# Adaptive-norm parts of one row instead of two at the head of a fused decoder step, one Trainium2 core

## The reference, cut to what matters

```python
mod = (jax.nn.silu(c) @ w_ada + b_ada)[:, None, :]      # w_ada (1024, 6 * 1024)
sh1, sc1, gt1, sh2, sc2, gt2 = jnp.split(mod, 6, axis=-1)
h = rms_norm(x, g1) * (1 + sc1) + sh1
z = h @ w_in                                            # u, q, k, v, ga, gb
u, q, k, v, ga, gb = jnp.split(z, IN_SPLITS, axis=-1)
# pooling branch on u, windowed attention on q, k, v, both gated, @ w_out
x = x + gt1 * (merged @ w_out)
h2 = rms_norm(x, g2) * (1 + sc2) + sh2
x = x + gt2 * (jnp.square(jax.nn.relu(h2 @ w_up)) @ w_down)
```

## Time and profile before

| | |
|---|---|
| median of three runs | 1281.45 us (1281.41 to 1281.77) |
| profiled execution | 1281.86 us |
| its span, first to last instruction | 1280.1 us |
| mean granted TensorE clock | 0.998 of full speed |
| TensorE busy | 98% of the span |
| VectorE, ScalarE, GpSimd busy | 70%, 44%, 15% |
| moved by DMA | 211.61 MB, 165 GB/s in the mean |

### The profile page before, as it was taken

The page is one execution under the profiler, slowest core; times in us unless marked ns, Lnnn a source line. Parts: engine busy times, 40 slices in busy tenths (PEclk is TensorE's granted clock), DMA queues, the critical chain, the costliest instruction groups (busy, mean ns, idle before and its releaser), DMA issues. The chain is left out here.

```text
span 1280.1 us, 25027 instructions
## 1 busy us (share of the span) xinstructions
PE 1254.5 (98%) x10261; PEld 1226.1 (96%) x10261; DVE 895.3 (70%) x1354; ACT 565.2 (44%) x982; POOL 193.4 (15%) x185
## 2 busy tenths in 40 slices
PE   6999999999999999999999999999999999999997
PEld 5999999999888999999999999999999999999996
DVE  6766655788775544347888886767678975688864
ACT  6433222254435333336856565545463434333252
POOL 2000002000000222221453333233210000000021
PEclk9999999999999999999999999999999999999999
DMA  9982343211125764454445554354598666776533
GB/s 325 328 278 67 101 141 116 81 37 59 47 64 176 233 216 134 146 148 117 132 128 183 156 156 155 126 166 126 183 333 281 199 204 198 221 251 193 182 122 102
DMA packets 241950, 211.61 MB, mean 165 GB/s; under 512 B 17489, under 2 KB 224213, under 8 KB 236957
## 3 DMA queue, kind: packets, MB, share of 16 engines
q1 hardware_dynamic: 240972, 209.67, 51.8%
q10 hardware_dynamic: 865, 0.36, 0.1%
HBM read 161.97 MB, written 49.04 MB: 165 GB/s over the span
## 5 line engine op out<-in xcount | busy, mean ns | idle before, releaser
L692 PE MATMUL psum<-xh,b_lo 128*128 128x264 f32 x908 | 257.8, 284 | 0.0
L690 PE MATMUL psum<-xh,b_hi 128*128 128x264 f32 x908 | 256.7, 283 | 0.0
L691 PE MATMUL psum<-xl,b_hi 128*128 128x264 f32 x908 | 256.2, 282 | 0.0
L690 PE MATMUL psum<-dh,e_hi 128*128 128x264 f32 x896 | 255.0, 285 | 0.0
L691 PE MATMUL psum<-dl,e_hi 128*128 128x264 f32 x896 | 253.9, 283 | 0.0
L692 PE MATMUL psum<-dh,e_lo 128*128 128x264 f32 x896 | 253.7, 283 | 0.0
L691 PEld LDWEIGHTS psum<-xl,b_hi 128*128 128x128 f32 x908 | 170.5, 188 | 0.0
L690 PEld LDWEIGHTS psum<-xh,b_hi 128*128 128x128 f32 x908 | 170.4, 188 | 0.0
L692 PEld LDWEIGHTS psum<-xh,b_lo 128*128 128x128 f32 x908 | 170.1, 187 | 0.0
L691 PEld LDWEIGHTS psum<-dl,e_hi 128*128 128x128 f32 x896 | 168.9, 188 | 0.0
L690 PEld LDWEIGHTS psum<-dh,e_hi 128*128 128x128 f32 x896 | 168.8, 188 | 0.0
(11 more groups left out here) (365 smaller groups left out, 2741.2 us busy)
## 6 DMA issues: line engine op xcount, KB each, us to landing
down_raw<-in_w_down_dram SPq DMA_DIRECT2D x72, 512.0 KB, 5.7
dr<-ff_scratch SPq DMA_DIRECT2D x28, 1056.0 KB, 8.3
up_raw<-in_w_up_dram SPq DMA_DIRECT2D x76, 256.0 KB, 3.9
ff_scratch<-st SPq DMA_DIRECT2D x64, 264.0 KB, 3.5
ff_scratch<-st SPq DMA_DIRECT2D x32, 396.0 KB, 3.7
g_in<-gates_scratch SPq DMA_DIRECT2D x8, 1056.0 KB, 5.9
ada_p<-in_w_ada_dram SPq DMA_DIRECT2D x8, 1024.0 KB, 12.5
ada_p<-in_w_ada_dram SPq DMA_DIRECT2D x4, 2048.0 KB, 11.9
```

The costliest lines, as they stand in the source:

```text
L690: mm(out, whi, rhi, start=first, stop=False)
L691: mm(out, whi, rlo, start=False, stop=False)
L692: return mm(out, wlo, rhi, start=False, stop=last)
```

## The change

The eight rows' shift and scale come in six parts instead of four pairs: rows 0, 1, 2, 3 alone, then rows 4 and 5, and 6 and 7. The first four parts take half of an `ada_p` buffer each, so none of their loads waits. The key weights are loaded ahead of the value weights, in two loads, both ahead of the second part. In TensorE's loop the matmuls of part k+1 stand after the third tile of unit 0 of row k, and its transpose after the first tile of unit 1, for k = 0 to 4. The samples' x block comes last, and their token scale has a spread and a copy of its own; `by_token` leaves them out, and `norm_samples` multiplies them itself, for one row at a time in the first four. VectorE multiplies each row by `R` in its own turn, and row 5's and 7's token products move. ScalarE's choice of rows for `nrm` stays.

```diff
-X_ORDER = (0, 1, 2, 3, 4, 5, 8, 6, 7)
+X_ORDER = tuple(range(9))
+ADA_P = ((0,), (1,), (2,), (3,), (4, 5), (6, 7))
+ADA_SLOT = (0, 0, 1, 1, 0, 1)
+def ada_of(k):
+    return next(e for e, js in enumerate(ADA_P) if k in js)
+def samples_of(k):
+    return k + 1 if k < 4 else 5 + (k - 4) // 2
+ADA_SEM = (0, 1, 2, 3, 0, 2)
...
@@ TensorE
-                if g == 2:
-                    last = mm(psum[:, g, n * P:TW[2]], ones[0:TS, :], diag1[0:TS, BLK, 0:TS], start=True, stop=True)
...
+            def spread_samples():
+                wait(pe, free[2], take(2, ("R", 3)))
+                pe.wait_ge(diag_done, 4)
+                mm(psum[:, 2, 0:TS], ones[0:TS, :], diag1[0:TS, BLK, 0:TS], start=True, stop=True).then_inc(ready[2], 1)
...
+            def part_rows(e):
+                pe.wait_ge(ada_in[ADA_SEM[e]], ada_landed(e))
+                ada_rows(("row", e), ADA_SLOT[e], (e % 2, 2 + e % 2) if e < 4 else range(4))
+            def part_turn(e):
+                ada_turn(("turned", e), ada_row[0:(2 * CW if e < 4 else P), e % 2, :], ("row", e))
...
             spread(2)
-            pair_rows(0)
-            pair_turn(0)
+            part_rows(0)
+            part_turn(0)
+            spread_samples()
             keep_busy(20)
             for k in range(DK):
-                if k in (1, 4):
-                    pair_rows(1 if k == 1 else 3)
                 for s in range(2):
-                    if (k, s) == (2, 1):
-                        pair_rows(2)
...
                             last.then_inc(ready[3 * s + t], 1)
-                        if (k, s, t) in ((1, 0, 0), (2, 1, 0), (4, 0, 0)):
-                            pair_turn({1: 1, 2: 2, 4: 3}[k])
+                        if k < 5 and (s, t) == (0, 2):
+                            part_rows(k + 1)
+                        if k < 5 and (s, t) == (1, 0):
+                            part_turn(k + 1)
 ScalarE
             r_copy(1)
             r_copy(2)
-            row_copy(("row", 0), 0, None)
             split_hi(0)
+            part_copy(0)
+            done = there(("R", 3))
+            fn(R[:, TP:T], psum[:, 2, 0:TS], ACT.Copy).then_inc(done, 1)
             for k in range(DK):
-                if k in (2, 4, 6):
-                    p = k // 2
-                    row_copy(("row", p), p % 2, ("turned", p - 2) if p >= 2 else None)
+                if k and k == ADA_P[ada_of(k)][0]:
+                    part_copy(ada_of(k))
                 act.wait_ge(xn_done, k + 1)
-                act.wait_ge(gain_done, k // 2 + 1)
+                act.wait_ge(gain_done, ada_of(k) + 1)
 VectorE
-                if p in (4, 7):
-                    diagonal(p // 3 - 1)
...
+                if p == 7:
+                    diagonal(1)
+                    diagonal(2)
+            mean_samples()
...
-                tt(xn[:, j, :], xT[:, j, :], R[:, :], ALU.mult).then_inc(xn_done, 1)
+                tt(xn[:, j, 0:TP], xT[:, j, 0:TP], R[:, 0:TP], ALU.mult).then_inc(xn_done, 1)
...
+                ch.step(tt(flat, xT[:, j, TP:T], R[:, TP:T].unsqueeze(1).to_broadcast([P, n, TS]), ALU.mult))
...
-            for j in range(2):
-                by_token(j)
-            pair_add(0)
+            by_token(0)
+            diagonal_samples()
+            part_add(0)
             norm(0)
             split_lo(0)
             norm_lo(0)
-            norm_samples(0)
+            norm_samples(0, 1)
             split_lo(1)
-            norm_lo(1)
-            for j in (2, 3):
+            for j in range(1, 4):
                 by_token(j)
+                part_add(j)
+                if j == 2:
+                    norm(j)
+                norm_lo(j)
+                norm_samples(j, 1)
+            for e in (4, 5):
+                j = ADA_P[e][0]
+                by_token(j)
+                part_add(e)
+                norm(j)
+                if e == 5:
+                    by_token(j + 1)
+                    norm(j + 1)
+                norm_lo(j)
+                norm_samples(j, 2)
+                if e == 4:
+                    by_token(j + 1)
+                norm_lo(j + 1)
 SP
+            def load_part(e):
+                j, n, slot = ADA_P[e][0], len(ADA_P[e]), ADA_SLOT[e]
+                if e >= 4:
+                    there(("row", 2 * e - 7))
...
-            load_pair(0)
-            sp.dma_start(kv_raw[:, :, :], w_in_d[:, z_col[0]:z_col[0] + 2 * P].rearrange("(k p) c -> p k c", p=P)).then_inc(w_in[0], 16)
-            for p in range(1, 4):
-                load_pair(p)
+            load_part(0)
+            for u in range(2):
+                sp.dma_start(kv_raw[:, :, u * P:(u + 1) * P], w_in_d[:, z_col[u]:z_col[u] + P].rearrange("(k p) c -> p k c", p=P)).then_inc(w_in[u], 16)
+            for e in range(1, 6):
+                load_part(e)
```

More of the change, by code:

```diff
@@ L547, in hybrid_decoder_step @@
         ms_done, rms_done, diag_done = sem("ms_done"), sem("rms_done"), sem("diag_done")
-        ada_in = [sem(f"ada_in{s}") for s in range(2)]
-        ada_rest = [sem(f"ada_rest{s}") for s in range(2)]
+        ada_in = [sem(f"ada_in{s}") for s in range(4)]
+        ada_rest = [ada_in[1], ada_in[3]]
         gain_done, xn_done = sem("gain_done"), sem("xn_done")
@@ L740, in _, with ada_rows @@
                     spread(p // 3 - 1)
-            def ada_rows(name, slot):
+            def ada_rows(name, slot, parts=range(4)):
                 wait(pe, free[6], take(6, name))
                 for k in range(DK):
-                    for q in range(4):
-                        last = mm(psum[CW * q:CW * q + CW, 6, 0:P], c_pad[:, k, :], ada_p[slot][:, k, q * P:(q + 1) * P], start=k == 0, stop=k == DK - 1)
+                    for r, q in enumerate(parts):
+                        last = mm(psum[CW * r:CW * r + CW, 6, 0:P], c_pad[:, k, :], ada_p[slot][:, k, q * P:(q + 1) * P], start=k == 0, stop=k == DK - 1)
                 last.then_inc(ready[6], 1)
@@ L758, in ada_turn @@
                 wait(pe, free[7], take(7, name))
-                nc.tensor.transpose(psum[:, 7, 0:P], row, ident[:, :]).then_inc(ready[7], 1)
+                n = row.shape[0]
+                nc.tensor.transpose(psum[:, 7, 0:n], row, ident[0:n, 0:n]).then_inc(ready[7], 1)
             def late_half(q):
@@ L1268, in _, with part_copy @@
             r_copy(2)
-            row_copy(("row", 0), 0, None)
+            def part_copy(e):
+                rows = 2 * CW if e < 4 else P
+                done = there(("row", e))
+                if e >= 2:
+                    there(("turned", e - 2))
+                fn(ada_row[0:rows, e % 2, :], psum[0:rows, 6, 0:P], ACT.Copy).then_inc(done, 1)
             split_hi(0)
+            part_copy(0)
+            done = there(("R", 3))
+            fn(R[:, TP:T], psum[:, 2, 0:TS], ACT.Copy).then_inc(done, 1)
             for k in range(DK):
-                if k in (2, 4, 6):
-                    p = k // 2
-                    row_copy(("row", p), p % 2, ("turned", p - 2) if p >= 2 else None)
+                if k and k == ADA_P[ada_of(k)][0]:
+                    part_copy(ada_of(k))
                 act.wait_ge(xn_done, k + 1)
-                act.wait_ge(gain_done, k // 2 + 1)
+                act.wait_ge(gain_done, ada_of(k) + 1)
                 fn(h_hi[:, k, 0:TP], xn[:, k, 0:TP], ACT.Identity, scale=gain1[:, k, 0:1], bias=mod[:, k, 0:1]).then_inc(n_hi, 1)
@@ L1288, in _ @@
             act.dma_start(inv_cnt[:, :, :].rearrange("p g c -> p (g c)"), a["inv_count"].partition_broadcast(P)).then_inc(tab_in, 16)
-            row_copy(("rest", 0), 0, ("turned", 2))
+            row_copy(("rest", 0), 0, ("turned", 4))
             def z_copy(u, t):
@@ L1331, in _ @@
                         n = REST_AT[i]
[L1332 removed]
+                        row_copy(("rest", n), n % 2, ("rturned", n - 2) if n >= 2 else ("turned", 4 + n))
                     for what in TX_ACT.get(i, ()):
@@ new lines, in _, with diagonal_samples, part_add @@
+                if p in (2, 5, 7):
+                    mean((2, 5, 7).index(p))
+                if p == 4:
+                    diagonal(0)
+                if p == 7:
+                    diagonal(1)
+                    diagonal(2)
+            mean_samples()
+            def diagonal_samples():
+                dve.wait_ge(rms_done, 4)
+                tt(diag1[0:TS, BLK, 0:TS], ident[0:TS, 0:TS], ssq[0:TS, BLK:BLK + 1].to_broadcast([TS, TS]), ALU.mult).then_inc(diag_done, 1)
+            def part_add(e):
+                done = there(("turned", e))
+                by_kind, add = mod[:, :, :].rearrange("p (a j) c -> p a j c", j=DK), vec[:, 0:NMOD].rearrange("p (a j) -> p a j", j=DK)
+                j, n = ADA_P[e][0], len(ADA_P[e])
+                js = slice(j, j + n)
+                tt(by_kind[:, 0:2, js, :], psum[:, 7, 0:2 * n * CW].rearrange("p (a j c) -> p a j c", a=2, j=n)[:, :, :, 0:NC],
+                   add[:, 0:2, js].unsqueeze(3).to_broadcast([P, 2, n, NC]), ALU.add).then_inc(done, 1)
```

(12 more changed lines are left out.)

64 lines of the change are left out of this document (20 added, 44 removed).

## The result

The changed kernel takes 1301.59 us in the median of four runs (1300.0 to 1303.52), beside 1281.61 for the kernel before: 1.0146 times the time (95% interval 1.0128 to 1.0164). The medians alone would give 1.0156, that is 20 us; the ratio on record gives 18.7. Either is slower, on the side that was forecast. The profiled execution took 1300.0 us, 18.1 over the one of before; its span is 1298.3.

A forecast was written before the change was run, and what follows sets the result against it. TensorE, busy 98% of the span, was taken to bound the kernel. Row starts summed to 44.4 us against 28.56 (+15.8); less 2.5 for the earlier start, +13.3 gave 1294.8 us on the median, range 1289.0 to 1302.5.

The forecast's parts named there:

- The link from turn to start: From a part's turn to TensorE's start of the next row: 3.44 us, with 1.14 more for rows 1 and 3.
- The start: Row 0's first `h_hi` matmul on TensorE at 27.2 instead of 29.71, so 2.5 us earlier.
- I take nothing, by the nearest row: Loads in 512-byte runs charged no extra time, since the stretch from 928 us showed 333 GB/s against 349.
- the bound (2.5): If short runs cost as much time as runs twice as long, the start's whole gain of 2.5 us is gone.
- Half a part takes half the time: Part matmuls on TensorE: 0.95 us for 32, against 1.89 for 64.
- The clock: Rival: clock falls in the stalls ahead of rows 1 and 3, adding 7.4 us, to 1302.2; chance 0.14.
- a granted clock under 1 in the head: Sign named in advance that would show the forecast wrong: the granted clock below 1 in the kernel's head.
- TensorE's busy time: TensorE's total busy time in the changed kernel goes up by 1 us only.
- Rows 5 to 7: Each row's start after the one before: 6.1, 5.4 and 2.97 us, with VectorE's order of work delaying rows 5 and 6.
- wait of 1 us for `ada_row` in row 4: TensorE stands about 1 us before part 5's turn, since ScalarE copies that part only after both its passes.
- The sum at row 7: Row 7's start on TensorE: rows add 15.8 us, the earlier start takes off 2.5, leaving 13.3 us later.
- later waits take it up: Rival: TensorE's seven later waits absorb 5.1 us of the delay, giving 1289.7; chance 0.10.

The follow-up runs named there:

- b_late: Kernel before, pairs kept, with only the matmuls and turns of pairs 1, 2 and 3 placed as late as in the changed kernel: 1292.24 us, ratio 1.0062.
- a_nrm: Changed kernel with the unsplit copy `nrm` of rows 1 and 3 made by VectorE instead of ScalarE: 1301.44 us, ratio 1.0129.
- b_short: Kernel before with each pair's two loads of 256 columns cut into four of 128, same bytes and order: 1288.23 us, ratio 1.0032.
- a_serial: Changed kernel with part matmuls ordered one 32-column strip after another, instead of strips in turn for each k: 1330.3 us in one profiled execution.
- a_warm: Changed kernel with filler transposes in TensorE's stalls ahead of rows 1, 2, 3, 4 and 6: 1295.25 us, ratio 1.0097.
- a_tail: Changed kernel with the edits of a_fill and a_nrm, plus VectorE's order for rows 4 to 7 as in the kernel before: 1288.21 us, ratio 1.0033.
- a_best: a_tail with part 1's matmuls after the first tile of row 0 and its turn after the third: 1286.40 us, ratio 1.0026.
- a_fill: Changed kernel with matmuls of parts 2, 3 and 4 moved into the stalls ahead of rows 1 to 3, turned early: 1291.07 us, ratio 1.0062.
- a_fill_nrm: Changed kernel with the edits of a_fill and a_nrm together: 1290.50 us, ratio 1.0048.

## Why the prediction was right or wrong

The side and the main mechanism were right. That the time lies in the range is in part luck: the forecast loss of 13.3 was a third too small, since two terms were missing or too small in it (half parts, clock), and the range reached up to 1302.5 only for a rival.

**The link from turn to start, right.** Forecast 3.44 for even rows and 4.59 for rows 1 and 3; measured 3.42 (42.39 to 45.81) and 3.44 (60.11 to 63.55), and 4.52 twice. b_late shows the place of the turn as the cause, a_nrm the second pass.

**The start, 0.65 short.** Row 0 at 27.86, not 27.2. The step that failed is the load rate: "I take nothing, by the nearest row". The stretch from 928 us had 333 GB/s of 512-byte runs of `w_down` mixed with `dr` loads of longer ones, so it was no measurement of short runs alone; those of `w_ada` and `w_in` give 289 to 295, and ScalarE's wait for the key weights ended at 22.67 where 21.6 was forecast. b_short shows the runs as the cause. It stayed within the bound (2.5) that was kept for it.

**Half a part takes half the time, wrong.** The term "0.95 for 32" measured 1.87: 0.92 more on the path of each of rows 1, 2 and 3, 2.8 in all. a_serial shows why. A hint stood in the rows: the 64 matmuls' 1.89 us are 30 ns each for 128 columns, while three of 384 columns (of another type, fp32r) took 0.62, some 60 to 70 ns per 128, which speaks for an overlap.

**The clock, a rival and not the forecast.** It had 0.14 and 1302.2; the kernel measured 1301.59. It came true and is one of the causes: three falls in the profile. By the prediction's own sign (a granted clock under 1 in the head) the forecast without it was wrong. But that the rival's number fits is luck: of its 7.4 us the clock made 3.6, and the half parts, which it didn't know, nearly 3 more. The lengths from a row's start to the turn are 5.79, 5.53 and 5.74 in the slow rows 1, 3 and 4, against 4.22 and 4.25 in rows 0 and 2, some 1.3 to 1.6 each. The price per fall (3.2 and 4.2) was too high, because the clock was back up after about 3 us, and the count (two) too low, since a stall of 2.24 did it as well. The two faster runs (1300.0 and 1300.9) have a mean clock of 0.994, the two slower ones (1302.3 and 1303.5) one of 0.992; whether they had more falls isn't shown, as only one was profiled.

**TensorE's busy time, wrong.** Forecast 1 us more, measured 10.6, all of it ahead of row 7. 3.8 are the two extra parts at 1.9 each, which is the half part again; an estimate from the three slow stretches (1.6, 1.3 and 1.5) gives 4.4 for the clock. The other 2.4 are not accounted for.

**Rows 5 to 7, nearly right.** Forecast 6.1, 5.4 and 2.97; measured 6.77, 4.66 and 3.09, and 5.96, 5.49 and 3.11 at full clock (a_warm). VectorE's order was the cause, as a_tail shows for row 6 (5.48 to 2.91). The forecast wait of 1 us for `ada_row` in row 4 did not appear, as the slow matmuls took its place; in a_warm, at full clock, it is there with 0.44.

**The sum at row 7.** Forecast 15.8 - 2.5 = 13.3, measured 21.65 - 1.85 = 19.8. The 6.5 between: start 0.65, half parts 2.8, clock some 3.6 in rows 2, 4 and 5, and -0.6 for rows 6 and 7. Later, 1.6 of the 19.8 comes back (span +18.2): before, TensorE waited 1.0 for an `ada_p` load and 0.5 for an `ada_l` load after 80 us. The changed kernel waits 0.2 in all for such loads, as TensorE comes later. The rival "later waits take it up" got this much right, at a third of its price; the other waits came back as they were.

**What brought the start forward was real** (1.85 to 2.5 us in all versions with single parts but a_serial) **and was never worth that at row 7**. In a_best rows 0 to 7 take 33.96 us for 28.56 before, 5.4 more: 3.8 are the two more parts, each with TensorE's 1.9, and 0.6 is a longer wait for `h_lo` (1.39 ahead of row 4, for 0.79 ahead of row 2). The remaining 1.0 isn't put down to a cause; what VectorE's samples, done six times instead of four, have in it was not tested alone. The rows that follow row 0 set the pace, not row 0.

## What to carry to other kernels

Work out the whole link from the instruction that gives a result to the one that needs it (here four instructions on three engines, 3.4 us), and compare it with the work queued between the two on the waiting engine: cutting a stage finer shortens neither the link nor a part's fixed time, and removes the cover. Before you halve a batch, see from its rows whether its pieces already run side by side. Price a stall on TensorE above its own length: where it is some 2 us (1.8 was the shortest here), add the slower clock that may follow, 1.3 to 1.6 us a time in the changed kernel.

## What the runs showed of the hardware

The granted clock fell to half after stalls of 1.82 us (a_fill, at 54 to 56), 1.97 (b_short, 22 to 28), 2.0 (a_nrm, 36 to 40), 2.2 (b_late, 40 to 44) and 3.1 (changed), and not after every such stall: it stayed at 1.00 behind the 2.01 ahead of row 2 in the changed kernel, behind 2.23 and 2.28 in b_late and behind 2.31 ahead of row 6 in a_fill_nrm. What decides between them isn't shown. The fall can come when TensorE is at work again: in the changed kernel row 1 starts at 36.60, and the granted clock is 1.00 until 37.0 and 0.50 from 37.5 to 40.5. The Trainium skill ("TensorE: Matmul & The Clock Gate", "HAM oscillation — how this bites in real kernels") gives as its abstract rule a limit for idle gaps that is higher than any of these stalls; the measurements show falls below it. With filler matmuls in the stalls the clock stayed at 1.00 (a_warm).

Loads of `w_ada` and `w_in` in runs of 512 bytes moved 289 to 295 GB/s (changed kernel, 18 to 34 us), in runs of 1 KB 347 to 352 (kernel before, 18 to 36). The Trainium skill ("DMA: Bandwidth & Descriptors", "Specifications") names 512 bytes as enough for line rate; here they were 17% below the runs of 1 KB.
